# Down projection of a ConvFFN: the residual block and the negated block go into PSUM ahead of two products

## The reference, cut to what matters

```
h = rmsnorm(x, norm_ffn_g)
gate, new_ffn = causal_dwconv(h @ w_gate, ffn_prev, conv_ffn_w, conv_ffn_b)
x = x + (silu(gate) * (h @ w_up)) @ w_down        # D_FF = 5632 rows, D_MODEL = 2048 columns
y = rmsnorm(x, final_norm_g)
```

## Time and profile before

| what | value |
|---|---|
| median of three runs | 2331.27 us (2330.81 to 2451.37) |
| the profiled execution | 2325.8 us, span 2324.1 us |
| granted TensorE clock in it, share of full speed | 0.992 |
| PE busy | 2269.7 us (98%) |
| DVE busy | 1692.8 us (73%) |
| ACT busy | 973.3 us (42%) |
| POOL busy | 545.1 us (23%) |

### The profile page before, as it was taken

The page is one execution under the profiler, slowest core; times in us unless marked ns, Lnnn a source line. Parts: engine busy times, 40 slices in busy tenths (PEclk is TensorE's granted clock), DMA queues, the critical chain, the costliest instruction groups (busy, mean ns, idle before and its releaser), DMA issues. The chain is left out here.

```text
span 2324.1 us, 43971 instructions
## 1 busy us (share of the span) xinstructions
PE 2269.7 (98%) x16978; PEld 2255.4 (97%) x16978; DVE 1692.8 (73%) x2283; ACT 973.3 (42%) x1469; POOL 545.1 (23%) x639
## 2 busy tenths in 40 slices
PE   7999999999999899999999999999999999999995
PEld 7999999999999899999999999999999999999995
DVE  6347745455422676888888888888888899898896
ACT  6224322223111344445444544444544554444454
POOL 2310000000222101111111111111112366656685
PEclk9999999999999999999999999999999999999998
DMA  7322232323533244454443444435446657755522
GB/s 244 100 78 63 74 92 73 90 72 105 169 107 106 66 137 122 128 160 132 135 150 128 154 130 142 148 119 163 129 138 221 209 198 243 230 198 194 185 78 100
DMA packets 368937, 320.09 MB, mean 138 GB/s; under 512 B 8649, under 2 KB 348740, under 8 KB 363073
## 3 DMA queue, kind: packets, MB, share of 16 engines
q1 hardware_dynamic: 346320, 203.98, 29.9%
q0 software_dynamic: 22512, 114.69, 13.3%
HBM read 258.32 MB, written 60.31 MB: 137 GB/s over the span
## 5 line engine op out<-in xcount | busy, mean ns | idle before, releaser
L1830 PE MATMUL ps<-h_hi,w_hi 128*128 128x288 f32 x1792 | 531.8, 297 | 2.2 <-issue 2.0
L1832 PE MATMUL ps<-h_hi,w_lo 128*128 128x288 f32 x1792 | 528.1, 295 | 0.0
L1831 PE MATMUL ps<-h_lo,w_hi 128*128 128x288 f32 x1792 | 528.1, 295 | 0.0
L2170 PE MATMUL ps<-form,dw_hi 128*128 128x288 f32 x1232 | 367.5, 298 | 12.4 <-DVE dw_lo L1718 10.9
L2171 PE MATMUL ps<-form,dw_hi 128*128 128x288 f32 x1232 | 363.0, 295 | 0.0
L2172 PE MATMUL ps<-form,dw_lo 128*128 128x288 f32 x1232 | 362.3, 294 | 0.0
L1830 PEld LDWEIGHTS ps<-h_hi,w_hi 128*128 128x128 f32 x1792 | 336.6, 188 | 3.5 <-issue 2.7
L1831 PEld LDWEIGHTS ps<-h_lo,w_hi 128*128 128x128 f32 x1792 | 336.6, 188 | 0.0
L1832 PEld LDWEIGHTS ps<-h_hi,w_lo 128*128 128x128 f32 x1792 | 336.5, 188 | 0.0
L1223 DVE TENSOR_TENSOR w_lo<-raw,w_hi 128x1024 fp32r<-128x1024 f32 x128 | 162.8, 1301 | 205.8 <-ACT w_hi L787 205.7
L1718 DVE TENSOR_TENSOR dw_lo<-down,dw_hi 128x512 fp32r<-128x512 f32 (+1 forms) x282 | 264.1, 950 | 47.1 <-ACT dw_hi L801 44.6
(11 more groups left out here) (289 smaller groups left out, 5178.7 us busy)
## 6 DMA issues: line engine op xcount, KB each, us to landing
raw<-in_w_gate_dram SPq DMA_DIRECT2D x88, 512.0 KB, 4.6
raw<-in_w_in_dram SPq DMA_DIRECT2D x80, 512.0 KB, 4.5
down<-in_w_down_dram SPq DMA_DIRECT2D x32, 1024.0 KB, 5.6
form<-act_scratch POOLq DMA_DIRECT2D x28, 1152.0 KB, 8.0
act_scratch<-stage POOLq DMA_DIRECT2D x46, 576.0 KB, 4.5
raw_c<-in_w_up_dram SPq DMA_DIRECT2D x40, 512.0 KB, 3.8
raw_d<-in_w_up_dram SPq DMA_DIRECT2D x40, 512.0 KB, 5.0
raw<-in_w_out_dram SPq DMA_DIRECT2D x32, 512.0 KB, 4.0
```

Source lines behind the costliest of these rows:

```text
L1830: te.matmul(out, whi, xhi, start=start, stop=False)
L1831: te.matmul(out, whi, xlo, start=False, stop=False)
L1832: return te.matmul(out, wlo, xhi, start=False, stop=stop)
L2170: te.matmul(out, dw_hi[:, m % 4, j, :], act_f[:, j, 0, :], start=start and j == 0, stop=False, skip_group_check=True)
```

## The change

From chunk 1 on, ACT copies the residual block `X[2gv, left]` into bank C ahead of product 2 (`fill_c`), and the negated block `X[2gv+1, left]` into bank D ahead of product 5 (`fill_d`). Products 2 and 5 then accumulate onto them (their `start` is false). In all 48 visits ACT takes bank D out into `X`, negated (`take_d`), where DVE's `sub_d` did it. POOL's `snap_add` 0 goes: `add_c` now adds the snapshot to bank C in every chunk. `bank_read` counts three a visit. PE waits for `c_filled` ahead of product 2 and for `d_filled` ahead of product 5 (below visit 40 it waited there for nothing, above it for `bank_read`); DVE's `add_a` waits for `d_read`. `fill_d` in visits above 40 waits for `add_a` of the visit before.

```diff
@@ pool
-                pool.wait_ge(bank_read, 4 * v + 4)
+                pool.wait_ge(bank_read, 3 * v + 3)
...
                 if v >= VISITS:
-                    pool.wait_ge(bank_read, 4 * (v - VISITS) + 4)
-                    snap_add(v, 0, p1_snap, 2 * gv, 0)
+                    pool.wait_ge(bank_read, 3 * (v - VISITS) + 3)
@@ scalar
-                if v > VISITS:
-                    act.wait_ge(snap_added, 3 * (v - 1 - VISITS) + n + 1)
+                if n >= 1 and v > VISITS:
+                    act.wait_ge(snap_added, 2 * (v - 1 - VISITS) + n)
                 elif v >= 1:
-                    act.wait_ge(bank_read, 4 * (v - 1) + (1, 4, 2)[n])
+                    act.wait_ge(bank_read, 3 * (v - 1) + (1, 3, 2)[n])
...
+            def fill_c(v):
+                gv = v % VISITS
+                act.wait_ge(bank_read, 3 * (v - 2) + 3)
+                if v > LAST_V:
+                    act.wait_ge(d_read, v)
+                if v // VISITS == X2_CHUNK + 1:
+                    act.wait_ge(x_back[gv], 16)
+                a.activation(ps[:, banks(v)[2], 0:HALF], X[:, 2 * gv, 0:HALF], ACT.Copy).then_inc(c_filled, 1)
+
+            def fill_d(v):
+                gv = v % VISITS
+                act.wait_ge(bank_read, 3 * (v - 1) + 3 if v > LAST_V else 3 * (v - 2) + 3)
+                a.activation(ps[:, banks(v)[3], 0:HALF], X[:, 2 * gv + 1, 0:HALF], ACT.Copy, scale=-1.0).then_inc(d_filled, 1)
+
+            def take_d(v):
+                act.wait_ge(piece_done, D0 + NQ * v + 6)
+                a.activation(X[:, 2 * (v % VISITS) + 1, 0:HALF], ps[:, banks(v)[3], 0:HALF], ACT.Copy, scale=-1.0
+                             ).then_inc(d_read, 1)
...
                 if v >= 1:
                     down_hi(m + 3)
+                if v >= VISITS:
+                    fill_c(v)
                 bank_snap(v, 0, 0, bank_a, p1_snap)
+                if v >= VISITS:
+                    fill_d(v)
                 down_hi(m + 4)
...
                 if more:
                     down_hi(m + 9)
+                take_d(v)
@@ vector
-            def sub_d(vi, j):
-                dve.wait_ge(piece_done, D0 + NQ * vi + 6)
-                xt, d = X[:, j + 1, 0:HALF], ps[:, banks(vi)[3], 0:HALF]
-                if vi < VISITS:
-                    v.tensor_scalar(xt, d, -1.0, None, ALU.mult).then_inc(bank_read, 1)
-                else:
-                    v.tensor_tensor(xt, xt, d, ALU.subtract).then_inc(bank_read, 1)
...
             def add_a(vi, j):
                 dve.wait_ge(piece_done, D0 + NQ * vi + 7)
-                dve.wait_ge(bank_read, 4 * vi + 3)
+                dve.wait_ge(d_read, vi + 1)
@@ tensor
-                    pe.wait_ge(bank_read, 4 * vi - 1)
-                down_product(vi, 2, bc, True, True)
+                if vi >= VISITS:
+                    pe.wait_ge(c_filled, vi - VISITS + 1)
+                down_product(vi, 2, bc, vi < VISITS, True)
...
-                    pe.wait_ge(bank_read, 4 * vi)
-                down_product(vi, 5, bd, True, True)
+                if vi >= VISITS:
+                    pe.wait_ge(d_filled, vi - VISITS + 1)
+                down_product(vi, 5, bd, vi < VISITS, True)
```

More of the change, by code:

```diff
@@ L231, in build_layer @@
         bank_read = sem("bank_read")
+        c_filled = sem("c_filled")
+        d_filled = sem("d_filled")
+        d_read = sem("d_read")
         b12_read = sem("b12_read")
@@ L1184, in _ @@
                 if v > LAST_V:
-                    last_tile(2 * gv - 1, 4 * v)
+                    last_tile(2 * gv - 1, 3 * v)
                 down_hi(m + 5)
@@ L1197, in _ @@
                 if v >= LAST_V:
-                    last_tile(2 * gv, 4 * v + 2)
+                    last_tile(2 * gv, 3 * v + 2)
                 if more:
                     down_hi(m + 9)
-            last_tile(KT - 1, 4 * VISITS * len(CHUNKS))
+                take_d(v)
+            last_tile(KT - 1, 3 * VISITS * len(CHUNKS))
             act.wait_ge(fssq_done, 1)
@@ L1745, in add_c @@
                 dve.wait_ge(piece_done, D0 + NQ * vi + 3)
-                if vi < VISITS:
-                    dve.wait_ge(p1_snap, vi + 1)
-                else:
-                    dve.wait_ge(snap_added, 3 * (vi - VISITS) + 1)
-                v.tensor_tensor(X[:, j, 0:HALF], snaps[:, 0, :] if vi < VISITS else X[:, j, 0:HALF], ps[:, banks(vi)[2], 0:HALF], ALU.add).then_inc(bank_read, 1)
+                dve.wait_ge(p1_snap, vi + 1)
+                v.tensor_tensor(X[:, j, 0:HALF], snaps[:, 0, :], ps[:, banks(vi)[2], 0:HALF], ALU.add).then_inc(bank_read, 1)
             def add_b(vi, j):
@@ L1756, in add_b @@
                 else:
-                    dve.wait_ge(snap_added, 3 * (vi - VISITS) + 3)
+                    dve.wait_ge(snap_added, 2 * (vi - VISITS) + 2)
                 v.tensor_tensor(X[:, j, HALF:T], snaps[:, 2, :] if vi < VISITS else X[:, j, HALF:T], ps[:, banks(vi)[1], 0:HALF], ALU.add).then_inc(bank_read, 1)
-            def sub_d(vi, j):
-                dve.wait_ge(piece_done, D0 + NQ * vi + 6)
-                xt, d = X[:, j + 1, 0:HALF], ps[:, banks(vi)[3], 0:HALF]
-                if vi < VISITS:
-                    v.tensor_scalar(xt, d, -1.0, None, ALU.mult).then_inc(bank_read, 1)
-                else:
-                    v.tensor_tensor(xt, xt, d, ALU.subtract).then_inc(bank_read, 1)
             def add_a(vi, j):
                 dve.wait_ge(piece_done, D0 + NQ * vi + 7)
-                dve.wait_ge(bank_read, 4 * vi + 3)
+                dve.wait_ge(d_read, vi + 1)
                 v.tensor_tensor(X[:, j + 1, HALF:T], snaps[:, 1, :] if vi < VISITS else X[:, j + 1, HALF:T], ps[:, banks(vi)[0], 0:HALF], ALU.add)
@@ L1801, in _ @@
                     out_store(j - 1, 1)
-                sub_d(vi, j)
                 if vi + 1 < NV:
@@ L2181, in out_t @@
                 else:
-                    pe.wait_ge(bank_read, 4 * LAST_V)
+                    pe.wait_ge(bank_read, 3 * LAST_V)
                 for b in range(TB):
@@ L2192, in _ @@
                 if vi > LAST_V:
-                    pe.wait_ge(bank_read, 4 * vi - 3)
+                    pe.wait_ge(bank_read, 3 * vi - 2)
                 elif vi >= 2:
-                    pe.wait_ge(bank_read, 4 * (vi - 1))
+                    pe.wait_ge(bank_read, 3 * (vi - 1))
                 down_product(vi, 0, ba, True, False)
                 if vi > LAST_V:
-                    pe.wait_ge(bank_read, 4 * vi - 2)
+                    pe.wait_ge(bank_read, 3 * vi - 1)
                 down_product(vi, 1, bb, True, False)
@@ L2206, in _ @@
                 if vi == 2:
-                    pe.wait_ge(bank_read, 8)
+                    pe.wait_ge(bank_read, 6)
                     states_t()
```

## The result

The changed kernel takes 2318.43 us (median of 7 runs, 2316.11 to 2321.81) against 2331.27 us before; the ratio is 0.9948, with a 95% interval of 0.9939 to 0.9958. By this ratio of the means the change wins 12.1 us, 0.5% (the two medians lie 12.8 us apart). That is under the 2% at which a change counts as faster here, but the interval leaves out 1. The profiled execution took 2317.66 us, span 2316.0. One of the runs before (2451.37 us) was disturbed and is left out of the ratio.

The account below looks back on a forecast made before the run. PE, busy 98% of the span, was taken as the bound, with near 13 us of waits to win. Gains of 0.3 + 1.5 + 2.0 + 2.5 = 6.3 us off 2331.3 gave 2325.0 us, range 2315 to 2338.

Parts of the forecast that it names:

- the case called the forecast: Whole kernel: 3 to 9 us faster, around a forecast median of 2325.0 us; chance 0.45.
- What bounds the kernel: Whole kernel: PE is busy 98% of the span; winning back its waits can give at most near 13 us.
- DVE loses `sub_d`, on the path only where DVE is: All 48 visits: 0.4 us less each, counting only in chunk 1, late rounds, chunk 5; chunk 0 gains 0.3, chunk 1 1.5.
- The 0.9 us wait for a form stays: Start of chunk 2: PE's 0.9 us wait remains, as POOL issues the load behind a snapshot that follows PE.
- Late rounds, 2.0 us: Waits behind visits 25 and 27: one queued POOL addition fewer at each, 1.24 + 0.78 us; bounds 0 to 4.6.
- Chunk 5, 2.5 us: Last seven visits: `fill_d` lengthens the loop 1.1 us, `sub_d` and shorter lo's outweigh it; gain halved to 2.5, between -4.5 and 5.2.
- PE's new waits and the fills in chunks 1 to 4: Chunks 1 to 4: ACT's fills and PE's waits on them cost nothing; bounds for the waits 0 to 0.1 us twice a visit.
- The range: Whole kernel: 2315 to 2338 us, all cases but the last, with the 4 or so us by which a median moves.
- lo m+8 near 0.7 us: Sign in chunk 5: DVE's lo m+8, 1.56 us before, falls near 0.7 because POOL is through its queue.
- DVE's idle ahead of lo m+5: Sign in chunk 5: DVE's idle there comes nearer 2 us than the 0.88 us before.
- the longer loop of chunk 5: Rival, chance 0.2: `fill_d` makes ACT's work wait for `add_a`, 0.7 us in each of seven visits; 2335.2 us.
- The port's rule in full: Rival, chance 0.13: each removed addition that met a lo frees its whole block, DVE waits of chunks 1 to 5 go; 2319.7 us.

Follow-up runs that it names:

- d_half: The changed kernel without `fill_c` and with POOL's third snapshot addition back, bank D's fill and take-out kept: 2325.24 us, ratio to before 0.9981.
- c_half: The kernel before with `fill_c` and two POOL snapshot additions a visit, `sub_d` kept: 2318.50 us, ratio to before 0.9950.
- before_gap: The kernel before with one POOL memset between second snapshot addition and weight sums, from the ninth visit on: 2328.84 us, ratio 0.9997.

## Why the prediction was right or wrong

The forecast of 6.3 us had the direction, and the time lies in the range, but the gain was twice as large: 12.1 us. That is outside the case called the forecast (3 to 9 us faster, chance 0.45); the case that came nearest had been given 0.13. The 2% called the least that can be told from no change was too coarse too: the interval is 0.2% wide. By its own terms, measured in the visits of PE:

- *What bounds the kernel*: right. PE's waits were the purse, "near 13 us", and 13.3 were won in the down projection of three profiles against two. But that the numbers agree is in part luck. The purse had been counted in one execution, and the other two took 2.7 and 3.4 us longer in the down projection, mainly in visits 9 and 28. It held 1.51 us in visit 0, counted among the small waits, which the change can't reach. And the gains below come in part from visits that had no wait in that list, such as 10 to 14.
- *DVE loses `sub_d`, on the path only where DVE is*: right for chunk 1, 1.5 us forecast and 1.86 measured; d_half shows that DVE's subtraction does it. (From 1884 to 1984 us, nearly all of chunk 1, DVE is busy 95% before, more than the 84 to 92% stated ahead of the prediction.) Of the 1.86, 1.1 come at 0.22 a visit as forecast and 0.76 from visit 15 alone (9.10 to 8.34), for which there was no term. Too small for chunk 0: 0.3 forecast, 2.0 measured, of which 1.4 in visit 3 and the rest in visit 0, where it is not the change's. In visit 3 `sub_d` stands in DVE's queue while DVE is behind; before, PE waits there twice, 0.42 and 0.27 us. Two kernels with `sub_d` in place and chunk 0 untouched, `c_half` and `before_gap`, have one of the waits only and take 9.15 and 9.53 us, so between 0.8 and 1.4 us are shown to be the subtraction's.
- *"The 0.9 us wait for a form stays"*: wrong, 0.9 us. I followed POOL's issue and not SP's, whose weight load is released by DVE and came 1.0 us earlier; the forms' landing follows it.
- *Late rounds, 2.0 us*: the term most off, 4.7 to 6.4 measured. The step that failed is that one of the five queued additions goes and the wait shortens by its length. One addition fewer, and the wait was gone, although four additions still follow each other without a gap: lo's of 3.78 and 5.71 us became ones of 1.42 us at most. The 5710 ns of the earlier trace rows could have told that a whole row passes a lo, but not that a row of four would not; the bound of 4.6 was the nearest value, and the rows before gave no reason to pick it.
- *Chunk 5, 2.5 us*: 2.4 measured, from parts of which some were wrong. Its own working gave 0.6 us a visit and 4.4 in all, and was halved for doubt; 0.4 a visit were won (13.34 to 12.95). `fill_d` on the loop: 1.1 us forecast, 1.0 measured (the square 1.19 us after `add_a` and not 0.19), and nothing with the fill moved. The two lo's after `add_c` fell from 3.07 to 1.28 us, far more than the 0.4 allowed. lo m+8 did not get shorter (1.47, forecast 0.64). And a wait not forecast came in, 0.77 us of `add_b` for POOL's last snapshot addition. That the sum came out is in part luck.
- *PE's new waits and the fills in chunks 1 to 4*: rightly put at nothing. Chunk 4 is at 11.11 us a visit, and a fill costs 0.40 us.
- *The range*: the 5.5 us between the profiled execution and the median were carried along as a constant. They are scatter of the kernel before: its two later profiles took 3.0 and 3.3 us longer than the first, nearly all of it in the down projection (visits 9 and 28), and the changed kernel lacks the late waits (its profile is 0.8 us from its median). The other 2 us or so stay open.

Of the signs, lo m+8 near 0.7 us did not come, and DVE's idle ahead of lo m+5 rose to 1.36 us only, with 0.43 more ahead of lo m+4. The others did.

Of the rivals, the longer loop of chunk 5 was there as a mechanism, and cost 2.95 us, but the relief outweighed it. The port's rule in full came nearest (2319.7 against 2318.4), partly by luck. It gave the waits after visits 25 and 27 as wholly gone, which is right, but by freeing one block, and the longest addition of that row before is 1.3 us where the lo was held for 5.71. It was wrong on chunk 5, where 5.2 us would have gone and 2.4 did.

## What to carry to other kernels

Look for the single instruction that is many times its median, and read what the neighbour engine does beside it from end to end: a row of POOL additions held one DVE instruction for the whole row, and one addition of 0.78 us fewer in each of two rows was worth 4.7 to 6.4 us. Such a gain can't be priced from the length of what is removed, so try it. When an instruction with a wait goes into an ordered queue, put it behind everything that does not need it; `fill_d` was done 4 us before PE wanted it (2271.03 against 2275.08 in visit 46) and cost 3 us in front of instructions that fed the critical loop. And take terms worked out from waits of one execution from several, before using them as a purse.

## What the runs showed of the hardware

- An instruction can be held for longer than one of the other engine's, both ways. One POOL addition of 288 columns, 0.78 us alone, took 2.52 us while DVE did two lo's and a weight sum back to back in chunk 5 of the changed kernel; a DVE lo of 0.68 us took 5.7 behind five POOL additions, and it had started 0.37 us ahead of the first of them (2064.34 against 2064.71 in the kernel before). At the start of the down projection two additions were enough, 2.60 us for a lo of 0.55. The Trainium skill's page "SBUF — State Buffer", section "Who interferes with whom", has the port held for one instruction and the other engine blocked for it. The same section has only POOL's reads contend with DVE's two-input instructions, and the runs agree (lo's of 0.68 and 0.69 us beside memsets). But a block of more than one instruction, and against the one that started first, is not in that rule; here the measurement decides. What decides whether the two engines take turns, as they do in chunk 1 and beside the four additions above, or one gets through a whole row, no run here told apart.
- ACT's copy from SBUF into PSUM took 398 and 411 ns for 288 columns, its copy out of PSUM 393: no difference that matters. Matmuls that accumulate onto a bank filled by ACT keep 0.132 us each.
